# A second block's column panels in another order, with softmax scaling and copies moved to ScalarE

## The reference, cut to what matters

```python
u = h @ w_in                      # 1024 -> z 2048, xbc 3072, dt 2*32, q/k/v 3*768, gates 2*1024
xbc = silu(centred_depthwise_conv(xbc, conv_w, conv_b))      # 5 taps
y = ssd forward + ssd backward + d_skip * x                  # state space, 32 heads of 64
y = y * silu(z); y = group_rms_norm(y) * ssd_norm_w          # 4 groups of 512
y_att = attention_branch(q, k, v) @ w_proj_attn              # 12 heads, 3 dilations, ALiBi
gates = sigmoid(gate_logits + b_gate)
mix = (gates[0] * (y @ w_proj_ssd) + gates[1] * y_att) @ w_out
h = layer_norm(alpha * h + mix); f = relu(h @ w_up)**2 @ w_down
h = layer_norm(alpha * h + f)
```

## Time and profile before

| | |
|---|---|
| median of 3 runs | 1238.55 us |
| the profiled execution, its span | 1241.7 us, 1239.9 us |
| PE busy | 1172.8 us (95%) |
| DVE busy | 911.4 us (74%) |
| ACT busy | 616.4 us (50%) |
| mean granted clock of PE | 0.978 |

### The profile page before, as it was taken

One profiled execution on the slowest core, in us unless ns is written; L12 is line 12 of the kernel. 1 busy time (PEld: TensorE's weight loads), 2 busy tenths in 40 slices (PEclk: granted clock), 3 DMA queues, 4 the chain that ended last, 5 costly groups with the idle time before them and its releaser, 6 DMA issues.

```text
span 1239.9 us, 19788 instructions
## 1 busy us (share of the span) xinstructions
PE 1172.8 (95%) x8054; PEld 1065.9 (86%) x8054; DVE 911.4 (74%) x1205; ACT 616.4 (50%) x814; POOL 58.0 (5%) x61
## 2 busy tenths in 40 slices
PE   3999999999999999999999998998989998999996
PEld 3978989999988888999999987887889996888885
DVE  6879798887778967756567479887984758656555
ACT  3753354444465436444444343568895734444441
POOL 1016000000000510000000000000000000000000
PEclk8899999999999999999999998999999999999998
DMA  9835467778765426555575532347864464455540
GB/s 380 357 151 204 178 234 296 279 265 307 262 230 204 170 69 220 199 173 197 173 262 204 170 136 103 109 163 238 257 221 137 167 241 170 165 178 201 186 152 34
DMA packets 44059, 249.35 MB, mean 201 GB/s; under 512 B 4352, under 2 KB 12672, under 8 KB 15952
## 3 DMA queue, kind: packets, MB, share of 16 engines
q1 hardware_dynamic: 43568, 246.19, 55.6%
q0 software_dynamic: 416, 2.11, 0.4%
HBM read 247.17 MB, written 1.11 MB: 200 GB/s over the span
## 4 chain that ended last, share of the span: by engine, by line
PE 78%; DVE 12%; ACT 5%; DMA 2%; issue 2%; SPq 0%; POOL 0%; DVEq 0%; ACTq 0%; POOLq 0%
PE bank L422 16%; PE bank L423 15%; PE bank L424 15%; PE bank L779 14%; PE bank L782 7%; PE bank L862 2%; DVE ring_w L417 2%; DMA raw<-in_panels 2%; DVE arena L2077 2%; PE bank L903 1%; ACT mixf L1896 1%; PE bank L761 1%; ACT mixf L1897 1%; PE bank L1683 1%; ACT w_hi L412 1%
## 5 line engine op out<-in xcount | busy, mean ns | idle before, releaser
L417 DVE TENSOR_TENSOR ring_w<-raw,w_hi 128x2048 fp32r<-128x2048 f32 x170 | 390.6, 2301 | 149.1 <-ACT w_hi L412 148.7
L412 ACT ACTIVATE w_hi<-raw 128x2048 fp32r<-128x2048 f32 x170 | 324.1, 1910 | 163.2 <-PE bank L424 152.7
L422 PE MATMUL bank<-act,w_hi 128*128 128x256 f32 x792 | 233.5, 295 | 6.0 <-DVE act L1180 2.7
L423 PE MATMUL bank<-act,w_hi 128*128 128x256 f32 x792 | 227.9, 288 | 0.0
L424 PE MATMUL bank<-act,ring_w 128*128 128x256 f32 x792 | 227.6, 287 | 0.0
L779 PE MATMUL bank<-act,w_hi 128*128 128x512 f32 x736 | 185.0, 393 | 0.2 <-DVE act L2214 0.2
L422 PEld LDWEIGHTS bank<-act,w_hi 128*128 128x128 f32 x792 | 155.7, 197 | 14.7 <-issue 12.3
L422 PE MATMUL bank<-ff_hi,w_hi 128*128 128x256 f32 (+1 forms) x560 | 157.7, 282 | 1.0 <-issue 1.0
L423 PE MATMUL bank<-ff_lo,w_hi 128*128 128x256 f32 (+1 forms) x560 | 158.2, 282 | 0.0
L424 PE MATMUL bank<-ff_hi,ring_w 128*128 128x256 f32 (+1 forms) x560 | 158.2, 282 | 0.0
L779 PEld LDWEIGHTS bank<-act,w_hi 128*128 128x128 f32 x736 | 134.0, 190 | 25.3 <-issue 0.6
(11 more groups left out here) (339 smaller groups left out, 1838.4 us busy)
## 6 DMA issues: line engine op xcount, KB each, us to landing
raw<-in_panels SPq DMA_DIRECT2D x170, 1024.0 KB, 4.9
arena<-in_modw SPq DMA_DIRECT2D x44, 1024.0 KB, 7.2
mixf<-dscr SPq DMA_DIRECT2D x8, 512.0 KB, 5.0
arena<-dscr SPq DMA_DIRECT2D x8, 512.0 KB, 5.1
mixf<-in_modw SPq DMA_DIRECT2D x2, 1024.0 KB, 16.4
act_flat<-in_modw SPq DMA_DIRECT2D x2, 1024.0 KB, 20.1
mixf<-dscr SPq DMA_DIRECT2D x8, 256.0 KB, 5.8
arena<-dscr SPq DMA_DIRECT2D x8, 256.0 KB, 6.2
```

The costliest lines, as they stand in the source:

```text
L412: nc.scalar.activation(w_hi[slot(k)][:, :], w_raw(m, k), ACT.Copy).then_inc(hi_done, 1)
L417: nc.vector.tensor_tensor(w_lo(m, k), w_raw(m, k), w_hi[slot(k)][:, :].bitcast(F32), ALU.subtract).then_inc(lo_done, 1)
L422: nc.tensor.matmul(o, wh, xh, start=start, stop=False, skip_group_check=skip)
L423: nc.tensor.matmul(o, wh, xl, start=False, stop=False, skip_group_check=skip)
```

## The change

The order of panels in the second block is written as three lists. Z is a z panel, X a convolution panel, G a gate panel; z panels 0 to 2 go between convolution panels, the attention's four gate panels into the state-space stage, the other four gates stay late. Where z is kept changes with it (`z_pair`): z panels come while the old z buffer still holds v and the probabilities. On DVE `normalized` keeps the reciprocal alone; ACT scales the probabilities (`scaled2`) and makes both copies to pt2. Squares get four buffers, and PE sums two groups behind each of the first two late panels. The step-size chain is spread over X0, X1 and the first two Z.

```diff
+CONV_PANELS = [("X", 0), ("X", 1), ("Z", 0), ("X", 2), ("X", 3), ("Z", 1), ("X", 4), ("X", 5), ("X", 6), ("Z", 2)] + [("X", j) for j in range(7, 12)]
+SSD_PANELS = [("Z", j) for j in range(3, 8)] + [("G", j) for j in range(4, 8)]
+LATE_PANELS = [("G", j) for j in range(4)]
+K_CONV, K_SSD, K_LATE = 9, 24, 33
...
         def finish(sp):
-            for k in range(6, 22):
+            for k in range(6, K_SSD + 3):
                 load(sp, M2, k)
-            load(sp, M2, 22)
-            load(sp, M2, 23)
...
# pe_second
-            for i in range(12):
-                panel2(9 + i)
-                if i == 5:
+            for p, (kind, i) in enumerate(CONV_PANELS):
+                panel2(K_CONV + p)
+                if kind == "Z":
+                    continue
+                if i == 8:
                     pe.wait_ge(dt_done, 1)
-                    pe.wait_ge(s2_ev0, 4)
+                    pe.wait_ge(s2_ev0, 6)
+                    pe.wait_ge(s2_ev1, 6)
...
+            for i in range(4):
+                panel2(K_LATE + i)
+                for n in ((0, 1), (2, 3), (), ())[i]:
                     pe.wait_ge(y_sq, n + 1)
...
# act_second
+            def scaled2(u):
+                act.wait_ge(s2_den, u + 1)
+                nc.scalar.activation(pp[u % 2], pp[u % 2], ACT.Copy, scale=dens2[:, u % 2:u % 2 + 1]).then_inc(s2_p, 1)
             exp2(0)
+            scaled2(0)
...
+            for p, (kind, i) in enumerate(CONV_PANELS):
+                k = K_CONV + p
+                if kind == "Z":
+                    take_z(k, i)
+                    split_hi(act, M2, k + 4)
+                    continue
...
                 if i in ATT_SLOT and ATT_SLOT[i] + 1 < 8:
                     exp2(ATT_SLOT[i] + 1)
...
-                split_hi(act, M2, 13 + i)
+                if i + 1 in ATT_SLOT:
+                    scaled2(ATT_SLOT[i + 1])
+                split_hi(act, M2, k + 4)
...
+                    nc.scalar.activation(pt2[:, 4:6, (u % 2) * P:(u % 2 + 1) * P], bank[7][:, 0:T].rearrange("p (n t) -> p n t", n=2), ACT.Copy)\
+                        .then_inc(s2_ev1, 1)
...
-            for n in range(2):
-                nc.scalar.activation(zb[:, 8 * n:8 * n + 8, :], zb[:, 8 * n:8 * n + 8, :], ACT.Silu).then_inc(z_silu, 1)
+            for v in (z4567, z01, z23):
+                nc.scalar.activation(v, v, ACT.Silu).then_inc(z_silu, 1)
             nc.scalar.preload_act_table_set("natural_log_exp_and_others")
+            take_gate(K_LATE - 1, 7, ga[:, 6:8, :])
+            split_hi(act, M2, K_LATE + 3)
             act.wait_ge(e_used, 16)
+            for n in range(4):
+                g = (2, 3, 0, 1)[n]
+                act.wait_ge(y_gated, n + 1)
+                nc.scalar.activation(sq2[n], xb[:, 4 * g:4 * g + 4, :], ACT.Square).then_inc(y_sq, 1)
+            for i in range(4):
+                take_gate(K_LATE + i, i, gb[:, 2 * i:2 * i + 2, :])
+                split_hi(act, M2, K_LATE + 4 + i)
...
# dve_second
             def normalized(u):
                 dve.wait_ge(s2_exp, u + 1)
-                link(nc.vector.reciprocal(dens2[:, u % 2:u % 2 + 1], dens2[:, u % 2:u % 2 + 1]))
-                nc.vector.tensor_scalar(pp[u % 2], pp[u % 2], dens2[:, u % 2:u % 2 + 1], None, ALU.mult).then_inc(s2_p, 1)
+                nc.vector.reciprocal(dens2[:, u % 2:u % 2 + 1], dens2[:, u % 2:u % 2 + 1]).then_inc(s2_den, 1)
...
+                if kind == "Z":
+                    if i < 2:
+                        dt_part(2 + i)
+                    split_lo(dve, M2, k + 4)
+                    continue
```

More of the change, by code:

```diff
@@ L1518, in build, with z_pair @@
         dtt = area(P, TT, 64)
-        gb = arena[:, xt_at:xt_at + 16 * T].rearrange("p (b t) -> p b t", b=16)
-        sq2 = arena[:, xt_at + 16 * T:xt_at + 20 * T].rearrange("p (b t) -> p b t", b=4)
-        rs2 = arena[:, xt_at + 20 * T:xt_at + 24 * T].rearrange("p (n t) -> p n t", n=4)
+        gb = arena[:, xt_at:xt_at + 8 * T].rearrange("p (b t) -> p b t", b=8)
+        sq2 = [arena[:, xt_at + (8 + 4 * n) * T:xt_at + (12 + 4 * n) * T].rearrange("p (b t) -> p b t", b=4) for n in range(4)]
+        rs2 = sq2[0]
+        ga = zb[:, 0:8, :]
+        z01 = mixf[:, 12 * T:16 * T].rearrange("p (b t) -> p b t", b=4)
+        z23 = ff_flat[:, :].rearrange("p (s q n) -> p s q n", s=2, q=2)[:, :, 1, :]
+        z4567 = zb[:, 8:16, :]
+        def z_pair(j):
+            if j < 2:
+                return z01[:, 2 * j:2 * j + 2, :]
+            if j < 4:
+                return z23[:, j - 2, :].rearrange("p (b t) -> p b t", b=2)
+            return z4567[:, 2 * j - 8:2 * j - 6, :]
         v2 = arena[:, zb_at:zb_at + 6 * T].rearrange("p (t n) -> p t n", t=TT)
@@ L1572, in finish @@
             fetch(sp, 1)
-            load(sp, M2, 24)
-            load(sp, M2, 25)
+            load(sp, M2, K_SSD + 3)
+            load(sp, M2, K_SSD + 4)
             sp.wait_ge(conv_done, 12)
@@ L1579, in finish @@
             for hu in range(8):
-                load(sp, M2, 26 + hu)
+                load(sp, M2, K_SSD + 5 + hu)
                 for e in (2 * hu + 4, 2 * hu + 5):
@@ L1585, in finish @@
                         fetch(sp, e)
-            for k in range(34, 46):
+            for k in range(K_SSD + 13, 46):
                 load(sp, M2, k)
@@ L1736, in pe_second @@
                     for b in range(4):
-                        last = nc.tensor.matmul(bank[6 + n // 2][:, n % 2 * T:(n % 2 + 1) * T], ones, sq2[:, b, :], start=b == 0, stop=b == 3)
+                        last = nc.tensor.matmul(bank[6 + n // 2][:, n % 2 * T:(n % 2 + 1) * T], ones, sq2[n][:, b, :], start=b == 0, stop=b == 3)
                     last.then_inc(y_ss, 1)
-                if i == 5:
+                if i == 3:
                     pe.wait_ge(y_out, 8)
@@ L1904, in act_second @@
             for hu in range(8):
-                used2(act, 21 + hu)
-                nc.scalar.activation(zb[:, 2 * hu:2 * hu + 2, :], blocks2(G2(21 + hu)[:, :]), ACT.Copy).then_inc(gfree[(21 + hu) % 2], 1)
+                kind, j = SSD_PANELS[hu]
+                if kind == "Z":
+                    take_z(K_SSD + hu, j)
+                else:
+                    take_gate(K_SSD + hu, j, ga[:, 2 * j - 8:2 * j - 6, :])
                 if hu < 7:
@@ L1915, in act_second @@
                     decay(2 * hu + 3)
-                split_hi(act, M2, 25 + hu)
+                split_hi(act, M2, K_SSD + 4 + hu)
             act.wait_ge(gfree[0], 9 * layers + 28 // 2 + 1 + 1)
             act.wait_ge(gfree[1], 9 * layers + 28 // 2 + 1)
-            for n in range(2):
-                nc.scalar.activation(zb[:, 8 * n:8 * n + 8, :], zb[:, 8 * n:8 * n + 8, :], ACT.Silu).then_inc(z_silu, 1)
+            for v in (z4567, z01, z23):
+                nc.scalar.activation(v, v, ACT.Silu).then_inc(z_silu, 1)
             nc.scalar.preload_act_table_set("natural_log_exp_and_others")
+            take_gate(K_LATE - 1, 7, ga[:, 6:8, :])
+            split_hi(act, M2, K_LATE + 3)
             act.wait_ge(e_used, 16)
[L1925 to L1938, removed]
+            for n in range(4):
[5 more added lines that the diff above has]
+                split_hi(act, M2, K_LATE + 4 + i)
+                if i == 1:
                     act.wait_ge(y_ss, 4)
@@ L1961, in act_second @@
             for n in (1, 0):
[L1962 removed]
+                nc.scalar.activation((gb, ga)[n], (gb, ga)[n], ACT.Sigmoid).then_inc(gates_done, 1)
             nc.scalar.preload_act_table_set("natural_log_exp_and_others")
@@ L2411, in lay_out @@
     z, xbc, dt_f, _, q, k, v, gates = [int(n) for n in N_SPLITS[:-1]]
-    cols = [n + 256 * j for n, count in ((q, 3), (k, 3), (v, 3), (xbc, 12), (z, 8), (gates, 8)) for j in range(count)]
+    first_col = dict(X=xbc, Z=z, G=gates)
+    cols = [n + 256 * j for n in (q, k, v) for j in range(3)] + [first_col[kind] + 256 * j for kind, j in CONV_PANELS + SSD_PANELS + LATE_PANELS]
     panels += [col_panel(w, slice(c, c + 256)) for c in cols]
```

70 lines of the change are left out of this document (40 added, 30 removed).

## The result

The changed kernel took 1244.63 us (median), 0.13 from the 1244.5 of the forecast; the ratio to the kernel before is 1.0043, interval 1.0026 to 1.0061. Run again beside more executions of the kernel before it took 1244.17, ratio 1.0053 [1.0032, 1.0074]. It is slower, by 5.8 us of the medians in the first set of runs and by 5.5 in the second. One execution of each kernel in the first set (1309.77 and 1659.90 us) took far longer than the rest and does not enter the ratio.

What follows compares the result with a forecast made beforehand. VectorE, making PE wait in the convolution stage, was taken as the bound. Convolution +2.0, state-space 0 and late +3.8 gave +5.8 on 1238.55: 1244.35, stated as 1244.5 us; range 1238 to 1248.5, leaving 2 in 10 out.

Steps and rivals of the forecast that it cites:

- The stands: Convolution stage: VectorE idles 2.8 us for ScalarE's scaling and split in seven steps before attention slots, 19 us in all.
- a price of 0.92: The Trainium skill's estimate in us for one scaling on ScalarE; the forecast took 0.84 instead.
- The pauses: PE waits: 0.6 us at the second slot, 3 before X5's PV, 3.5 before X10's transposes, 5.0 before the sums of squares.
- the first rival: Convolution stage: z panels give VectorE time that absorbs the stands, as totals say; 1232.5 us; chance 0.10.
- The 1.0 for issue: Late stage: PE's 1.0 us pause before the attention projection goes, since the transposes of x cover the last gate.
- The low clock: Time lost to slow PE clock behind pauses: 2.3 us at X5, 3.1 after X10, 3.1 in the late stage.
- the 3.72 row: Kernel before, convolution stage: PE's 3.72 us pause before the transposes at 767.53, with about 3.1 us lost beside it.
- The second rival: Each of the three long pauses costs only 1.4 us of low clock: +1.5, 1240.0 us; chance 0.26.
- The third: Rival: scaling costs 0.28 more per chain and low clock after the late pause loses 5 us: +9, 1247.5 us; chance 0.14.
- The loss in the kernel before: Convolution stage before: pauses of 3.7, 1.9 and 0.4 plus low clock of 3.1 and 1.4, 10.5 us to win.
- State-space stage: Longer gates on ScalarE hide behind its wait for VectorE's masks: no change, 0.5 us if the cover failed.
- Median and profile: The profiled execution of before took 1241.7 us, 3.15 above the median 1238.55; the forecast was shifted to the median's scale.

Runs made afterwards that it cites:

- the one edit that turns two instructions round: Changed kernel with ScalarE splitting the next panel's weights before it scales the probabilities: 1233.04 us, ratio 0.9960 to the kernel before.
- the move alone: Kernel before, its panel order kept, with scaling (ahead of the split into w_hi) and both copies on ScalarE: 1250.25 us, ratio 1.0086.
- the run with the reordered queue: Changed kernel, late stage only: last gate before the Silus, weight split behind the squares, sums of squares one panel later: 1241.51 us; again 1238.99 us.
- the fill: Changed kernel with idle matmuls, results unused, in PE's three long pauses: 1242.83 us, ratio 1.0033 to the kernel before.

## Why the time was right and two of its terms were not

**The stands, VectorE's idle time before the split: right.** Seven of 2.8 us, 19 in all, were summed; the trace has 20.4, seven near 2.8 and one of 0.75. The scaling was taken at 0.84 from start to start and takes 0.84 (800.57 to 801.41). The prediction's remark that by a price of 0.92 every chain would be 0.08 longer sets an instruction's duration against a step: the row lasts 0.94, and the next instruction starts 0.84 after it. That the stands make the pauses is shown by the one edit that turns two instructions round (-10.4 in the stage), and by the move alone (+10.7).

**The pauses: right.** 0.6, 3, 3.5 and 5.0 were summed; 0.55, 3.04, 3.53 and 5.08 stand. Each came from following one engine's queue from a known start, instruction by instruction, to what PE waits for. Totals would have misled: DVE's work fits with room, and that was the first rival. In the late stage the run with the reordered queue shows that ScalarE's order makes the pause, but not which of its instructions. The 1.0 for issue ahead of the attention projection went, as forecast.

**The low clock: mis-sized.** This is the step that failed: "For the low clock I take 3.1 after X10 (next to the 3.72 row) and 2.3 at X5", with 3.1 late, 8.5 in all. Measured were 1.5, 1.6 and 2.2, 5.3 in all, and for the late one the fill gives 2.1. The step took the loss to go by the length of the pause. The runs don't bear that out: 3.53 cost 1.5 here and nothing in one of the experiments, 3.72 cost 3.1, 5.08 cost 2.2, 1.9 cost 1.4 to 1.5 or nothing. Hence the convolution stage, for which +2.0 was forecast, changed by -0.4, and the late stage by +3.3 (+3.8 forecast); against the first profile of before, from which the forecast was made, by -0.9 and +2.8. The second rival, 1.4 per pause, was nearer on this term, 4.2. The third, 5 us lost behind the late pause, is out.

**The loss in the kernel before: read too low.** The prediction summed 10.5 us that the convolution stage could win. The stage without any pause takes 101.9, which is 11.9 below the 113.7 of that profile. A part of it is a misreading: for the transposes behind the pause of 1.86 it took 0.8, but here no scores follow, and from start to start (821.47 to the row below) they take 0.6. So that pause cost 1.5 to 1.6, not 1.4; the rest I can't place.

```profile
822.07 0.36 PE L422 MATMUL bank<-act,w_hi 128*128 128x256 f32 x1
```

**State-space stage: right, at nothing** (78.43 against 78.53).

**What the prediction didn't have: +1.6 from panel 38 on.** The pause of 2.0 us for VectorE's mix_lo stands in both kernels; after the change the clock falls behind it, in the kernel before it doesn't (after, then before):

```profile
1024.50:1029.00 4.50, 4.50 (x14) 3.51 (x14) 4.17 (x7) 2.15 (x3) 0.00 (x0) 0.62 0.46 193
```

```profile
1024.50:1029.00 4.50, 4.50 (x20) 3.73 (x21) 4.33 (x7) 1.99 (x3) 0.00 (x0) 1.00 0.48 202
```

The three profiles of before have 263.5 or 263.6 us from panel 38 on, the eleven of the other kernels 263.8 (once) and 264.9 to 265.4. The kernel with the move alone has 265.2, though its code is that of before in that part, and the two profiles of the late stage reordered have 265.3 and 263.8 with the same code. So it isn't the code of that part. Why it is so regular stays open.

**Median and profile.** The prediction subtracted 3.15 because the profiled execution lay so far above the median, and left the change's worth untouched. Two of before's three profiles are of that kind, and both of after's lie at its median or below; so the stages show +3.4 where the medians differ by 5.5. About 2 us I can't place. The time came out by luck: a low clock priced 3.2 too high stood in for the 1.6 that was not foreseen and most of these 2. The stands and the pauses are shown; the agreement to 0.13 us is not merit.

## What to carry to other kernels

When work moves to another in-order engine, look at what it is put ahead of: an instruction that waits for its partner engine should not stand in front of one that the partner needs. Two instructions turned round were worth 11 us here, and which engine did the scaling some 0.6. Sum such chains by queue, not by totals. Price a pause as itself plus a low clock behind it that cost nothing to 3 us in these runs, and don't take it as a proportion of the pause.

## What the hardware showed that was not expected

Low clock can cost nothing. In the changed kernel the clock falls at 902 us, in the state-space stage (0.50 from 902.5 to 905). PE waits there for VectorE's masks at each step; behind the slow stretch the next wait is 0.30 instead of 1.8:

```profile
901.62 1.54 PE L1746 MATMUL bank<-mixf,arena 128*64 128x256 f32 x8 [1.83 <-DVE mixf L2165]
...
921.05 1.08 PE L1746 MATMUL bank<-mixf,arena 128*64 128x256 f32 x8 [0.30 <-DVE mixf L2165]
```

In the kernel with the filled pauses the clock stays up there, and the same wait is 1.83:

```profile
922.74 1.08 PE L1756 MATMUL bank<-mixf,arena 128*64 128x256 f32 x8 [1.83 <-DVE mixf L2179]
```

The stage takes 78.43 and 78.44 us. At X6 it is the same: where the clock is low behind X5, PE comes later and doesn't wait the 1.7 for VectorE. In these places a loss of clock counted only as far as PE was what the stage waited for.
